# Attention scores from three products of 64 contraction rows for each map, in the two row halves of the array

## What is computed

```python
H, Dh = 4, 64                      # four heads, each with two maps of 64 channels
qf = q.astype(jnp.float32) * (dh ** -0.5)
scores = jnp.einsum("bqhmd,bkhmd->bhmqk", qb, kf)     # m: the two maps
scores = jnp.where(causal, scores, -jnp.inf)
p = jax.nn.softmax(scores, axis=-1)
a = p[:, :, 0] - lam * p[:, :, 1]
return jnp.einsum("bhqk,bkhe->bqhe", a, vf)
```

## Time and profile before

| | before |
|---|---|
| median of 3 runs | 2504.31 us (2502.43 to 2512.29) |
| the profiled execution | 2498.92 us |
| its span | 2497.1 us |
| mean granted clock of PE | 0.987 of full speed |
| PE busy | 2360.2 us |
| PEld busy | 1936.9 us |
| DVE busy | 1474.4 us |
| ACT busy | 791.7 us |
| POOL busy | 374.8 us |
| HBM traffic | 193 GB/s over the span |

### The profile page before, as it was taken

How to read it: one execution, slowest core, us unless ns; L and a number is a source line. 1 busy time by engine, 2 the same in 40 slices (tenths; PEclk the granted TensorE clock), 3 DMA queues, 4 the chain that set the end, 5 groups by cost and what they waited for, 6 DMA issues and landing times.

```text
span 2497.1 us, 30297 instructions
## 1 busy us (share of the span) xinstructions
PE 2360.2 (95%) x11272; PEld 1936.9 (78%) x11272; DVE 1474.4 (59%) x2940; ACT 791.7 (32%) x1754; POOL 374.8 (15%) x296
## 2 busy tenths in 40 slices
PE   7999999989999999999999999999998989899997
PEld 5777778768777778878877778887887777778886
DVE  4777755473666664453666667455366666575652
ACT  3433332242323331021444344102144444341020
POOL 3545454341000000010000000001000000000010
PEclk9999999999999999999999999999999999999999
DMA  7777678768444445555644443555554343334544
GB/s 264 250 248 257 230 265 293 248 243 300 173 156 169 160 156 177 199 202 202 238 175 155 157 172 133 182 189 217 205 219 146 134 153 133 127 119 169 191 175 183
DMA packets 86641, 484.53 MB, mean 194 GB/s; under 512 B 8928, under 2 KB 9184, under 8 KB 41440
## 3 DMA queue, kind: packets, MB, share of 16 engines
q1 hardware_dynamic: 86496, 482.60, 54.8%
HBM read 369.32 MB, written 113.25 MB: 193 GB/s over the span
## 4 chain that ended last, share of the span: by engine, by line
PE 79%; DVE 11%; issue 3%; ACT 3%; POOL 2%; DMA 1%; SPq 0%; POOLq 0%; ACTq 0%; DVEq 0%
PE PJ L552 58%; PE SC L599 5%; PE OB L660 5%; PE SC L628 5%; PE TB L639 2%; DVE ZA L1147 1%; DMA Wp<-split_weights 1%; POOL Wp L987 1%; PE PJ L599 1%; PE OB L599 1%; DVE ACCS L1268 1%; DVE PX L1140 1%; DVE ZA L1189 1%; DVE negm L1102 1%; PE TB L666 1%
## 5 line engine op out<-in xcount | busy, mean ns | idle before, releaser
L552 PE MATMUL PJ<-hT,Wp 128*128 128x512 f32 x6528 | 1598.9, 396 | 3.7 <-DVE hT L1095 3.1
L552 PEld LDWEIGHTS PJ<-hT,Wp 128*128 128x128 f32 x6528 | 1206.5, 189 | 244.0 <-DVE hT L1095 3.5
L1268 DVE SCALAR_TENSOR_TENSOR ACCS<-UA,col,ACCS 128x512 f32<-128x512 f32 x464 | 389.3, 870 | 0.8
L987 POOL TENSOR_TENSOR Wp<-Wraw,Wp 128x1024 fp32r<-128x1024 f32 x88 | 217.5, 2472 | 290.7 <-ACT Wp L748 290.7
L832 ACT ACTIVATE PX<-SC,negm 128x512 f32<-128x512 f32 (+3 forms) x320 | 196.5, 621 | 172.3 <-DVE negm L1102 172.1
L1102 DVE TENSOR_REDUCE negm<-SC 128x2 f32<-128x1024 f32 (+3 forms) x160 | 169.5, 1060 | 88.8 <-PE SC L632 48.3
L852 ACT ACTIVATE ZA<-TB 128x512 fp32r<-128x512 f32 (+3 forms) x160 | 85.4, 534 | 326.7 <-PE TB L639 325.8
L628 PE MATMUL SC<-KM,ZA 128*128 128x512 f32 (+3 forms) x640 | 164.1, 374 | 18.5 <-issue 17.6
L1147 DVE TENSOR_TENSOR ZA<-TB,ZA 128x512 fp32r<-128x512 f32 (+3 forms) x160 | 97.3, 608 | 128.4 <-ACT ZA L852 127.8
L1000 POOL TENSOR_TENSOR ost<-ost,nhalf 128x1 f32<-128x1 f32 x64 | 50.9, 795 | 798.2 <-DVE ost L1163 798.2
L886 ACT ACTIVATE TG<-PJ,col 128x512 f32<-128x512 f32 x64 | 44.0, 688 | 378.5 <-PE PJ L552 378.5
(11 more groups left out here) (172 smaller groups left out, 2103.5 us busy)
## 6 DMA issues: line engine op xcount, KB each, us to landing
Wp<-split_weights SPq DMA_DIRECT2D x264, 1024.0 KB, 4.8
split_weights<-Wp SPq DMA_DIRECT2D x88, 1024.0 KB, 4.8
Wraw<-w_stream SPq DMA_DIRECT2D x88, 512.0 KB, 5.7
KM<-keys SPq DMA_DIRECT2D x24, 512.0 KB, 4.3
VM<-values SPq DMA_DIRECT2D x24, 512.0 KB, 4.6
PX<-x SPq DMA_DIRECT2D x4, 2048.0 KB, 7.9
out<-PX SPq DMA_DIRECT2D x16, 512.0 KB, 6.9
keys<-KM SPq DMA_DIRECT2D x12, 512.0 KB, 3.5
```

Of the source, the lines that this page charges most:

```text
L552: mm = pe.matmul(PJ[bank(r)][:, :], wt, rhs[:, 1 if q == 1 else 0, k, :], start=(n == 0), stop=(n == 3 * ktiles - 1))
L987: pool.tensor_tensor(Wp[:, k, 1, :], Wraw[:, w % 2, :], Wp[:, k, 0, :].bitcast(F32), ALU.subtract).then_inc(w_lo, 1)
L1268: a = dve.scalar_tensor_tensor(out=acc, in0=src, scalar=col[:, n:n + 1], in1=acc, op0=ALU.mult, op1=ALU.add)
```

## The change

The operands are laid out as they are projected: partition `64 m + d` holds channel `d` of map `m`, both for queries and for keys. `QM` has two slots, hi and lo, instead of four; `KM` has hi in its first and lo in its second half. So each of the four splits is one instruction of 128x512. A map's score now has a contraction over 64 rows only, and takes three products: hi by hi, hi by lo and lo by hi. The products of map 0 use array rows 0 to 63, those of map 1 rows 64 to 127, and they alternate. A unit has six products in place of four. The mask's products stand together behind them.

```diff
--- before.py
+++ after.py
@@ -269,7 +269,8 @@
         PX = sb("PX", [P, 2, KB, 2, CHUNK])
         xres = PX[:, 1, :, :, :].rearrange("p t m n -> p t (m n)")
         ZA = sb("ZA", [P, 2, KB, CHUNK], F32R)
-        QM = ZA[:, 0, :, :]
+
+        QM = ZA[:, 0, 0:2, :]
         AT = ZA[:, 1, :, :].rearrange("p (u a) (b n) -> p u a b n", u=2, n=P)
         ZB = sb("ZB", [P, 2, KB, CHUNK], F32R)
         ZC = sb("ZC", [P, 2, KB, CHUNK], F32R)
@@ -623,12 +624,14 @@
                 if t == 0 and j < c:
                     pe.wait_ge(k_loaded[j], 16 * (loads_before(c, h, j) + 1))
                 wait(pe, sc_free[k], score_use(c, h, t, j))
-                for m in range(2):
-                    for q in range(2):
-                        mm = pe.matmul(SC[k][:, m, 0:w], QM[:, 2 * q + m, t * P:(t + 1) * P],
-                                       KM[:, m, j * CHUNK:j * CHUNK + w], start=(q == 0),
-                                       stop=(q == 1 and j < c))
-                    if j == c:
+                for n, (ql, kl) in enumerate(((0, 0), (0, 1), (1, 0))):
+                    for m in range(2):
+                        rows = slice(64 * m, 64 * m + 64)
+                        mm = pe.matmul(SC[k][:, m, 0:w], QM[rows, ql, t * P:(t + 1) * P],
+                                       KM[rows, kl, j * CHUNK:j * CHUNK + w], start=(n == 0),
+                                       stop=(n == 2 and j < c))
+                if j == c:
+                    for m in range(2):
                         mm = pe.matmul(SC[k][:, m, w - P:w], identb[:, :], maskb[:, :], start=False, stop=True)
                 mm.then_inc(qk_done, 1)
 
@@ -765,11 +768,7 @@
                 wait(act, qk_done, unit(c, h, 0, 0))
                 if h == 0:
                     wait(act, group_done, G_CHUNK * c)
-                for m in range(2):
-                    for half in range(2):
-                        a = act.activation(QM[64 * half:64 * half + 64, m, :], PJ[bank(r)][64 * m:64 * m + 64, :],
-                                           ACT.Copy, scale=QSCALE)
-                a.then_inc(qk_hi, 1)
+                act.activation(QM[:, 0, :], PJ[bank(r)][:, :], ACT.Copy, scale=QSCALE).then_inc(qk_hi, 1)
 
             def key_hi(c, h):
                 r = head_group(h, K_)
@@ -779,10 +778,7 @@
                     wait(act, fin_done, WO_T * c)
                 elif c < NCHUNK - 1:
                     act.wait_ge(k_stored, 16 * head_at(c, h))
-                for m in range(2):
-                    a = act.activation(KM[0:64, m, c * CHUNK:(c + 1) * CHUNK], PJ[bank(r)][64 * m:64 * m + 64, :],
-                                       ACT.Copy)
-                a.then_inc(qk_hi, 1)
+                act.activation(KM[:, 0, c * CHUNK:(c + 1) * CHUNK], PJ[bank(r)][:, :], ACT.Copy).then_inc(qk_hi, 1)
 
             def value_hi(c, h):
                 act.wait_ge(v_turned, head_at(c, h) + 1)
@@ -1183,20 +1179,15 @@
             def query_lo(c, h):
                 r = head_group(h, Q_)
                 dve.wait_ge(qk_hi, 2 * head_at(c, h) + 2)
-                for m in range(2):
-                    for half in range(2):
-                        ps = slice(64 * half, 64 * half + 64)
-                        a = dve.scalar_tensor_tensor(out=QM[ps, 2 + m, :], in0=PJ[bank(r)][64 * m:64 * m + 64, :],
-                                                     scalar=QSCALE, in1=QM[64 * m:64 * m + 64, m, :].bitcast(F32),
-                                                     op0=ALU.mult, op1=ALU.subtract)
+                a = dve.scalar_tensor_tensor(out=QM[:, 1, :], in0=PJ[bank(r)][:, :], scalar=QSCALE,
+                                             in1=QM[:, 0, :].bitcast(F32), op0=ALU.mult, op1=ALU.subtract)
                 a.then_inc(pj_free[bank(r)], 1)
 
             def key_lo(c, h):
                 r = head_group(h, K_)
                 dve.wait_ge(qk_hi, 2 * head_at(c, h) + 1)
-                for m in range(2):
-                    a = dve.tensor_tensor(KM[64:128, m, c * CHUNK:(c + 1) * CHUNK], PJ[bank(r)][64 * m:64 * m + 64, :],
-                                          KM[0:64, m, c * CHUNK:(c + 1) * CHUNK].bitcast(F32), ALU.subtract)
+                a = dve.tensor_tensor(KM[:, 1, c * CHUNK:(c + 1) * CHUNK], PJ[bank(r)][:, :],
+                                      KM[:, 0, c * CHUNK:(c + 1) * CHUNK].bitcast(F32), ALU.subtract)
                 a.then_inc(pj_free[bank(r)], 1)
 
             def value_lo(c, h):
```

## The result

| | before | changed |
|---|---|---|
| median, 5 runs each | 2502.43 us | 2482.22 us |
| all runs | 2500.14 to 2512.29 | 2480.67 to 2487.39 |
| the profiled execution (that of the kernel before is none of the five) | 2498.92 us | 2480.67 us |
| mean granted clock of PE there | 0.987 | 0.991 |

The ratio is 0.9919, with a 95% interval of 0.9895 to 0.9943: 20 us faster, 0.8%. I had forecast 2455 us. On another chip, beside 17 runs of the kernel before, the same changed kernel came to 0.9941 (0.9924 to 0.9959).

What follows compares the result with a forecast made beforehand. PE was taken as the bound. From the profiled 2498.9 us, 27 us for the splits and 23 us for the products came off, giving 2449; the runs' median stands 5.4 us higher, so 2455 us, range 2440 to 2545.

Steps and rivals of the forecast that it cites:

- What PE waits for before scores: Before scores, PE's 12 waits, 17.6 us, are for the split of the query, not its own issue; all go.
- The price of the splits: On ACT and DVE, one instruction each of 0.60 and 0.70 us replaces four; shorter waits give PE 27 us.
- Side by side: In PE's scores, both halves run together: six products take 0.68 us at 512 wide, not 0.91; products give 23 us.
- The change of form at nothing: On PE, 320 switches between products of 128 and 64 rows cost nothing; upper bound 0.28 us each.
- Rival A: PE drains at each switch between 128 and 64 rows, 54 to 90 us: 2509 to 2545 us; chance 0.25.
- its point of decision: Price per switch of product rows on PE, 0.16 us, from which on it decides against the change: (27 + 23) / 320.
- rival B: In PE's scores, the two halves don't overlap, products cost 64 us: 2541 us; chance 0.12.
- the narrow units' 13 us: Cost of PE's 48 narrower units if their six products run one after another, about 13 us.

Runs made afterwards that it cites:

- two units together: Changed kernel with scores of units 0 and 1, and of 2 and 3, of a tile issued together on PE: 2474.43 us (0.9880); repeated, 2472.19 us (0.9876).
- map by map: Changed kernel with another order within a unit, the three products of map 0 and then the three of map 1: 2491.63 us, ratio 0.9941.

## Why the prediction was wrong

It had the direction; the size was 50 us where 20 came (15 on the second chip), and 2455 us lies far below the runs. By its steps:

- **What PE waits for before scores: right.** It was the query's split. With it in one piece each the waits are gone in every kernel that has it, and the 17.6 us return to the tenth with the slow splits.
- **The price of the splits: right.** 0.60 and 0.70 us were forecast, 0.60 and 0.68 came. 27 us of waits were to go, 28.7 us went by the page. By the runs the splits alone are worth 34 us; some 5 us of this are the clock by the estimate above, and some 28 are left.
- **Side by side: right.** Both halves run at once: one pair costs what one half product costs, and the two products of a pair start 0.003 us apart (1904.831 and 1904.834 in the unit above). Without the edges a unit would take 0.68 us.
- **The change of form at nothing: this step failed.** It was the term with bounds of 0 and 0.28 us where I took 0, "since nothing in the rows stops for a change of form". 0.20 to 0.23 us is the measured size, at 512 columns. The products were to give 23 us and cost 16.5 us instead, some 20 at the same clock: 40 us or a little more apart. For a unit off the diagonal the rows above give 0.90 - 0.68 = 0.22 us within it, 0.32 - 0.23 = 0.09 ahead of it and 1.03 - 0.91 = 0.12 behind it, 0.43 us more than forecast; over 96 units that is 41 us. The whole forecast missed by less, 27 us in the time. By the estimates above the clock gave something that stood in no term: at the same clock the change is worth some 8 us by its two halves and some 11 by its own runs on the second chip. What came above that was luck.
- **Why the miss isn't 320 x 0.21 = 67 us.** On the diagonal it is smaller. My estimate there had six loads one after another, 0.74 us at 128 columns; they go in pairs, and the unit took 0.58. A change between narrow products costs 0.15 us and not 0.2; and behind the mask's short product the next load was exposed before as well: four projection products took 1.17 us there, against 1.07 behind a plain unit. Measured in both traces from the last projection product ahead of a unit to the third behind it, medians of the units with projection products on both sides, a unit off the diagonal takes 1.79 us against 1.59 before, 0.20 us more (65 units); on the diagonal it is 0.17, 0.10, 0.04 and 0.00 us more at 128, 256, 384 and 512 columns.
- **Rival A** had the price right (0.17 to 0.28 us) and its point of decision, 0.16 us, wrong: by it the change would have been slower. It let the whole price fall on all 320 changes. (In rival B the narrow units' 13 us should be 15, since the masks' 0.08 us were taken off once too often; nothing hangs on it.)

The rows that misled me were those of the mask, 128 rows wide as everything else, which say nothing of a change of rows. And I misread them: "no sign of a price" is not what they show. Behind the mask four projection products took 1.17 us and not 1.07, and eight took 2.10 and 2.08 us where seven paces and a product make 1.98; behind the float32 turns too the second projection product follows after 0.315 us (1922.377 and 1922.692 in the trace of before). So some 0.1 us behind narrow products was there to see, and nothing was not a bound that the rows gave.

"TensorEngine Tiling (Array Packing)" of the Trainium skill, section Tiling Modes, had the rule that decided, that a change of tiling mode drains TensorE. The trace agrees in that nothing of the new form, product or load, starts until 0.32 us after the last product of the old form started; that PE is empty by then it does not show, since that product's record ends 0.07 us later and ends are modelled. The price is about 0.2 us: 0.09 us until the new form's first product, and then 0.11 us of load that lie open before each side gets back to its pace.

Open is the clock. The median over a kernel's runs was 0.985 or 0.987 for the kernel before and 0.9885 or 0.990 for the changed one; the share that shows in the time could be 4 to 8 us. What brings it about was not found. Neither fewer waits nor products of 64 rows are needed for it: the products alone, with the waits of before, ran at 0.9864 against 0.9848, and the splits alone, with products of 128 rows, at 0.9870; the two kernels with another order of the splits and products of 128 rows, the second of them with 7 us less of waits, ran lower than the one before.

## What to carry to other kernels

Products on the two halves of the array's rows really run two at a time, but each switch between whole-array and half-array products costs about 0.2 us of PE: an excursion into half-array products must save more than 0.4 us, so gather as many of them as the buffers allow (two units together gave back some 10 to 15 us by the ratios, and 17 us against map by map on one chip). When a bound in an estimate runs from nothing to a price that is multiplied by 320, take a value between, or make the forecast depend on it, and ask which rows really show the thing that changes. And a split, copy or other small step on the chain between two engines is worth shortening by making it fewer instructions; starting it earlier in the same full queues gave nothing, and with a new order in them the wait moved and a quarter of a per cent came. Last, when a change is worth under 1%, compare the mean granted clock of the runs: here about 2.2 to 2.5 us went with each 0.001.

## What the hardware showed that I had not expected

Products on the two halves of the array start out of the program's order: a product of the next pattern started 0.44 us before an earlier one on the other half (2520.55 against 2520.99), and three by three, the two maps ran side by side. The reach was about three products: eight and eight took 2.96 us, not 1.8, and the second eight began with three of the first still to start. And two weight loads for the two halves start together and take 0.18 us like one: six loads of a unit went in 0.53 us (1904.83 and on), where I had allowed for six times 0.11, 0.66 us.
